# Products of a tile of ones in TensorE's waits, in an encoder trunk of one layer

## What is computed

```python
u = rms_norm(x, attn_norm) @ w_in
y_h = hyena_mixer(u[..., :1536], ...)            # short conv, two long convolutions by FFT, gates
y_a = mla_mixer(u[..., 1536:1792], u[..., 1792:1920], u[..., 1920:], ...)   # 8 heads of attention
y = rms_norm(concatenate([y_h, y_a]).reshape(B, L, 2, 512), out_norm.reshape(2, 512))
x = x + y @ w_out
x = x + ec_moe(rms_norm(x, mlp_norm), w_router, w_gate, w_up, w_down)
```

## Time and profile before

| what | value |
|---|---|
| median of 3 runs | 2699.3 us (2695.45 to 2703.31) |
| the profiled execution's own time | 2694.75 us |
| its span | 2693.0 us |
| TensorE busy | 2466.5 us, 92% of the span |
| mean granted clock of TensorE | 0.949 of full speed |

### The profile page before, as it was taken

One profiled execution on the slowest core, in us unless ns is written; L12 is line 12 of the kernel. 1 busy time (PEld: TensorE's weight loads), 2 busy tenths in 40 slices (PEclk: granted clock), 3 DMA queues, 4 the chain that ended last, 5 costly groups with the idle time before them and its releaser, 6 DMA issues. The chain is left out here.

```text
span 2693.0 us, 50844 instructions
## 1 busy us (share of the span) xinstructions
PE 2466.5 (92%) x19983; PEld 1381.6 (51%) x19983; DVE 1898.6 (71%) x2630; ACT 1640.7 (61%) x2314; POOL 1145.8 (43%) x1032
## 2 busy tenths in 40 slices
PE   6899999879999999998898989799944999999997
PEld 4555555436666666663332233355433666666664
DVE  5547767647777777776898989566646677777773
ACT  6734455338888888887654855343434666666651
POOL 1224344226666666666403900234312355544431
PEclk9999999969999999998899989899965999999999
DMA  7403345344311211125796888755544899999972
GB/s 191 132 34 129 111 141 175 116 86 158 111 41 42 48 41 44 30 53 192 255 331 213 291 285 294 209 160 158 157 148 115 273 270 275 276 259 258 271 189 51
DMA packets 391771, 445.10 MB, mean 165 GB/s; under 512 B 206159, under 2 KB 270415, under 8 KB 389265
## 3 DMA queue, kind: packets, MB, share of 16 engines
q1 hardware_dynamic: 367056, 369.78, 44.9%
q0 software_dynamic: 12288, 38.05, 5.9%
q10 hardware_dynamic: 12224, 34.48, 3.7%
HBM read 267.72 MB, written 137.91 MB: 151 GB/s over the span
## 5 line engine op out<-in xcount | busy, mean ns | idle before, releaser
L1276 POOL TENSOR_TENSOR at_p<-at_pf,at_p 128x512 f16<-128x512 f32 x325 | 378.6, 1173 | 260.7 <-ACT at_p L1411 260.3
L1552 DVE TENSOR_REDUCE at_mxs<-at_pM 128x1 f32<-128x512 f32 x512 | 344.0, 688 | 102.1 <-PE at_pM L1442 100.2
L1410 ACT ACTIVATE at_pf<-at_pS,at_scale 128x1024 f32<-128x1024 f32 x260 | 289.8, 1115 | 107.7 <-PE at_pS L1473 103.1
L1411 ACT ACTIVATE at_p<-at_pS,at_scale 128x1024 f16<-128x1024 f32 x260 | 287.8, 1107 | 0.0
L1498 PE MATMUL at_pO<-at_vv,at_p 128*128 128x65 f16 x2080 | 226.8, 194 | 2.8 <-POOL at_p L1276 2.8
L1499 PE MATMUL at_pO<-at_vv,at_p 128*128 128x64 f16 x2080 | 226.1, 195 | 0.0
L1501 PE MATMUL at_pO<-at_vv,at_p 128*128 128x65 f16 x2080 | 225.6, 193 | 0.0
L1499 PEld LDWEIGHTS at_pO<-at_vv,at_p 128*128 128x128 f16 x2080 | 195.1, 98 | 37.3 <-issue 0.8
L1442 PE MATMUL at_pM<-at_kT,at_qT 96*128 96x512 f16 x512 | 199.3, 391 | 15.6 <-DMA at_qT<-s_QK 12.4
L1498 PEld LDWEIGHTS at_pO<-at_vv,at_p 128*128 128x128 f16 x2080 | 195.2, 97 | 34.6 <-issue 3.0
L1471 PE MATMUL at_pS<-at_qT,at_kT 97*128 97x512 f16 (+1 forms) x528 | 201.5, 382 | 3.3 <-DMA at_qT<-at_nmx 2.2
(11 more groups left out here) (427 smaller groups left out, 6210.1 us busy)
## 6 DMA issues: line engine op xcount, KB each, us to landing
s_F<-fs_a SPq DMA_DIRECT2D x72, 512.0 KB, 3.2
sp_rows<-s_F SPq DMA_DIRECT2D x72, 512.0 KB, 5.7
mo_raw<-in_w_gate SPq DMA_DIRECT2D x32, 1024.0 KB
mo_raw<-in_w_up SPq DMA_DIRECT2D x32, 1024.0 KB
mo_down<-in_w_down SPq DMA_DIRECT2D x32, 1024.0 KB, 5.0
s_QK<-pj_R ACTq DMA_DIRECT2D x18, 1024.0 KB, 3.9
s_G<-sp_gg SPq DMA_DIRECT2D x72, 256.0 KB, 4.3
sp_tab<-tab_spec SPq DMA_DIRECT2D x72, 224.0 KB, 4.2
```

Of the source, the lines that this page charges most:

```text
L1276: eng.tensor_tensor(p2[r][:, half, :], pf[:, r, half, :], p1[r][:, half, :], ALU.subtract).then_inc(own_done if own(g, half) else others_d ...
L1410: act.activation(pf[:, r, :, :], pS[g % 2][:, :, :], ACT.Exp, scale=scale[:, 0:1])
L1411: act.activation(p1[r][:, :, :], pS[g % 2][:, :, :], ACT.Exp, scale=scale[:, 0:1]).then_inc(p_made, 1)
L1552: dve.tensor_reduce(mxs[:, j // NC, j % NC:j % NC + 1], pM[j % 2][:, :], AX.X, ALU.max).then_inc(pM_free, 1)
```

## The change

A helper `keep_awake(pe, out, of, n)` issues `n` products of a tile of ones by itself, 128 x 128 by 128 x 128 in float32, into a PSUM region that nobody reads at that time. None of them signals a semaphore. It runs at 30 points of TensorE's stream and at 13 more in the rounds of `choose` (there with 8 products), and `attend` gets a tile of ones and a semaphore for it. Some of the calls are preceded by a wait for the last reader of the region that they write. Counted over the program it is 965 products. Nothing is removed or moved.

The diff, with the unchanged lines mostly left out:

```diff
--- before.py
+++ after.py
@@ -250,6 +250,12 @@
         TAKEN.append(nc.alloc_semaphore(prefix + name))
...
     return sem
+
+
+def keep_awake(pe, out, of, n):
+
+    for _ in range(n):
+        pe.matmul(out, of[:, :], of[:, :], start=True, stop=True)
 
...
 def clear_semaphores(nc):
@@ -818,10 +824,13 @@
                     last = pe.matmul(pF[:, m, 0:c1 - c0], (w1, w2)[n][:, :], (feats, h1)[n][:, c0:c1], start=True, stop=True)
...
 
+            pe.wait_ge(consts, 4)
+            keep_awake(pe, pC[:, 0:P], ones, 50)
             pe.wait_ge(gain_in, 32)
             turn_x(0)
-            pe.wait_ge(consts, 4)
+            keep_awake(pe, pC[:, 0:P], ones, 10)
             add_squares("c", C_PARTS)
+            keep_awake(pe, pC[:, 0:P], ones, 26)
             turn_x(1)
...
                 if 1 < t + 1 < NT:
@@ -899,6 +908,8 @@
                     make_q(m)
...
                     make_k(m)
+            pe.wait_ge(u_moved, SLOTS)
+            keep_awake(pe, pU[0][:, 0:P], ones, 46)
 
...
         def _(dve):
@@ -1193,6 +1204,7 @@
         q1, q2, k1, k2 = ([x[:, m, :] for x in both] for both in (qT, kT) for m in range(2))
...
         zero = sb("zero", [P, 1])
+        ones = sb("ones", [P, P])
         scale = sb("scale", [P, 1])
...
         mxs = sb("mxs", [P, TQ, NC])
@@ -1207,7 +1219,7 @@
         pS = [ps(f"pS{r}", [P, 2, 512]) for r in range(2)]
...
 
-        consts, eye_in, ready = sem("consts"), sem("eye_in"), sem("ready")
+        consts, eye_in, ready, ones_made = sem("consts"), sem("eye_in"), sem("ready"), sem("ones_made")
         q1_in, q2_in, k1_in, k2_in = ([sem(f"{n}_in{b}") for b in range(2)] for n in ("q1", "q2", "k1", "k2"))
...
         v_in, v_split = sem("v_in"), sem("v_split")
@@ -1364,6 +1376,7 @@
 
...
         def _(pool):
+            pool.memset(ones[:, :], 1.0).then_inc(ones_made, 1)
             pool.memset(zero[:, :], 0.0).then_inc(ready, 1)
...
                 pool.memset(vv[b][:, :, 0:1], 1.0).then_inc(ready, 1)
@@ -1412,6 +1425,8 @@
 
...
         def _(pe):
+            pe.wait_ge(ones_made, 1)
+            keep_awake(pe, pM[0][:, 0:P], ones, 44)
             pe.wait_ge(ready, 3)
...
             def slot(h, b, qb, j):
@@ -1511,6 +1526,7 @@
 
...
                 lead(*leading(0, 0, n))
+            keep_awake(pe, pS[0][:, 0, 0:P], ones, 12)
             for g in range(LAG):
...
             for g in range(NS * NH + NSS):
@@ -1535,6 +1551,8 @@
                         slot(of_h, of_b, of_qb, tiles[2])
...
                     turn_max(of_h, of_qb)
+            pe.wait_ge(pM_free, slots_before(NH, NQ))
+            keep_awake(pe, pM[1][:, 0:P], ones, 38)
 
...
         def _(dve):
@@ -1686,6 +1704,7 @@
             sem("last_in"), sem("topped"), sem("normed"), sem("inverted"))
...
         hidden_in, cleared, z_made, z_moved = sem("hidden_in"), sem("cleared"), sem("z_made"), sem("z_moved")
+        ones_made = sem("ones_made")
         z_out, a_out = ([sem(f"{n}_out{b}") for b in range(2)] for n in "za")
...
         Z_LAG = LAG if closes else 0
@@ -1809,6 +1828,8 @@
         @block.tensor
...
             if order == 0:
+                pe.wait_ge(ones_made, 1)
+                keep_awake(pe, pZ[:, 0, 0:P], s["ones"], 24)
                 pe.wait_ge(hidden_in, 32)
...
 
@@ -1823,6 +1844,8 @@
                     last = pe.matmul(pH[:, d, :], s["hidden"][side, rows(i)], w3[side, :], start=True, stop=True)
...
                 if closes:
+                    if i == 0:
+                        keep_awake(pe, pZ[:, 0, 0:P], s["ones"], 14)
                     pe.wait_ge(g_in[i % GB], 16 * (i // GB) + 16)
...
                         pe.wait_ge(closed, 2 * (i - 2) + 1)
@@ -1878,12 +1901,14 @@
                 if i == NT:
...
             norms(1)
+            pe.wait_ge(z_moved, (1 + closes) * NT)
+            keep_awake(pe, pZ[:, 0, 0:P], s["ones"], 28 if closes else 42)
 
...
             if order == 0:
-                dve.memset(s["ones"][:, :], 1.0)
+                dve.memset(s["ones"][:, :], 1.0).then_inc(ones_made, 1)
 
...
                 dve.memset(s["hidden"][FH:, 0:1], 0.0).then_inc(cleared, 1)
@@ -2122,6 +2147,7 @@
                 last.then_inc(g_made, 1)
...
             pe.matmul(pSum, s["ones"][:, :], s["sizes"][:, :], start=True, stop=True).then_inc(summed, 1)
+            keep_awake(pe, pX[0][:, 0:P], s["ones"], 40)
             pe.wait_ge(totalled, 2)
...
                 forward(n)
@@ -2129,6 +2155,8 @@
                     backward(n - LAG)
...
                 backward(n)
+            pe.wait_ge(x_moved, STEPS)
+            keep_awake(pe, pX[0][:, 0:P], s["ones"], 36 if order else 24)
 
...
         def _(dve):
@@ -2541,10 +2569,13 @@
 
...
             pe.matmul(pW, ones[:, :], w_sum[:, :], start=True, stop=True).then_inc(w_summed, 1)
+            keep_awake(pe, pU[:, 0:P], ones, 15)
             invert(0)
+            keep_awake(pe, pU[:, 0:P], ones, 48)
             pe.wait_ge(eye_in, 16)
...
             invert(1)
+            keep_awake(pe, pU[:, 0:P], ones, 8)
             for t in range(NT):
...
                     invert(t + 2)
@@ -2557,8 +2588,11 @@
                     turn_y(t + 1)
...
                     route(t - 1)
+            pe.wait_ge(chain, 2 * NT)
+            keep_awake(pe, pV[:, 0:P], ones, 28)
             turn_x(NT - 1)
             route(NT - 1)
+            keep_awake(pe, pV[:, 0:P], ones, 28)
 
...
         def _(dve):
@@ -2812,7 +2846,8 @@
         pP = ps("pP", [P, 512])
...
         pO = [ps(f"pO{g}", [P, 512])[:, 0:2 * P].rearrange("p (s b e) -> p s b e", s=2, b=16) for g in range(2)]
-        pF = ps("pF", [P, 512])[:, 0:NC * E_N].rearrange("p (c e) -> p c e", c=NC)
+        pF_bank = ps("pF", [P, 512])
+        pF, spare = pF_bank[:, 0:NC * E_N].rearrange("p (c e) -> p c e", c=NC), pF_bank[:, 0:P]
 
...
         loaded, turned, chain, exps = sem("loaded"), sem("turned"), sem("chain"), sem("exps")
@@ -2866,6 +2901,8 @@
 
...
         def _(pe):
+            pe.wait_ge(consts, 1)
+            keep_awake(pe, spare, weights["ones"], 20)
             pe.wait_ge(loaded, 32)
...
             for n in range(4):
@@ -2909,15 +2946,21 @@
 
...
             pe.wait_ge(consts, 3)
+            keep_awake(pe, spare, weights["ones"], 26)
             for n in range(ROUNDS):
...
                     add_squares(pe, weights, pN[:, 0:W_PARTS], 0)
+                elif n < ROUNDS - 1:
+                    keep_awake(pe, spare, weights["ones"], 8)
             pe.wait_ge(tabs_in, 48)
+            keep_awake(pe, spare, weights["ones"], 20)
             pe.wait_ge(picked, 1)
             rank(tied, tied_sum, over_sum)
+            keep_awake(pe, spare, weights["ones"], 8)
             pe.wait_ge(picked, 2)
             rank(taken, taken_sum, nothing)
+            keep_awake(pe, spare, weights["ones"], 62)
             pe.wait_ge(placed, 1)
...
                 n, of, first, last_t = (P, 0, 0, NP - 1) if t < NP else (H, 1, NP, NP + NS - 1)
@@ -2926,6 +2969,7 @@
                     last = pe.matmul(pO[g][:, of, :, :], in_a[0:n, t, g, :, :].rearrange("p a e -> p (a e)"), in_b[0:n, t, g, :, :],
...
             last.then_inc(spotted, 1)
+            keep_awake(pe, spare, weights["ones"], 14)
             pe.wait_ge(spread_made, 1)
...
                 for g in range(2):
@@ -3442,16 +3486,21 @@
                     add_h(e - 1)
...
                 product(e, b, 1, 0)
-                if not begins(e):
+                if begins(e):
+                    keep_awake(pe, pY[0][:, 0:P], weights["ones"], 28)
+                else:
                     down(e - 1)
...
                 product(e, b, 2, 1)
+                if begins(e):
+                    keep_awake(pe, pY[0][:, 0:P], weights["ones"], 8)
                 if more == 2:
...
                 product(e, b, 3, 1)
+            keep_awake(pe, pG[1][:, 0:P], weights["ones"], 46)
             pe.wait_ge(eye_made, 1)
...
                 at = 2 * CAPS[1] if c == 2 else 0
@@ -3463,6 +3512,8 @@
                     add_squares(pe, weights, pN, 1)
...
             add_h(E_N - 1)
+            pe.wait_ge(y_ready, 2 * NC * (E_N - 1))
+            keep_awake(pe, pY[0][:, 0:P], weights["ones"], 28)
             down(E_N - 1)
```

## The result

The changed kernel takes 2752.7 us (median of 4 runs, 2749.3 to 2755.9), the kernel before 2699.9 us in the same session (4 runs). The ratio is 1.019, 95% interval 1.0166 to 1.0213. I had forecast 2726 us, with a range to 2748: the direction was right, the size was not. The profiled execution of the changed kernel took 2752.57 us, with a span of 2750.8 us.

A forecast was written before the change was run, and what follows sets the result against it. TensorE, busy 92% of the span, was taken to bound the kernel. Costs of 61 us less gains of 33 gave +28 on 2694.75 us: 2723, or 2727 as a median, given as 2726; range 2690 to 2748.

The forecast's parts named there:

- the price of a product: Each inserted float32 product on TensorE: two records, 0.214 us warm and 0.427 us cold.
- The rival of one record: A product is one record of 0.107 to 0.13 us, so nearly every group fits: 25 us faster, 2674; chance 0.12.
- The costs, place by place: Products ending later than what TensorE waits for, at stage starts, ends and inner waits: 61 us in all.
- the 46 of the experts: At the experts' start, 46 products take 9.8 us in a wait of 7.2: +4 us.
- What warm work gives back: TensorE work on the chain that ran at half clock gets faster: 33 us together, of a bound of 70.
- `attend`'s opening: Start of `attend`, 19 us busy at low clock, paced by VectorE's maxima: gain of 4 of at most 9 us.
- the starts of filters, spectra and merge: First steps of `filters`, `spectra` (twice) and `merge` gain about 2.5 us each, second `filters` 1: together 11.
- the rounds and ranks: In `choose`, counts behind the last mask shorten 0.2 us a round, 3 in all; ranks and placings give 4.
- the first expert: TensorE's work in the first expert, run warm, gives back 6 us.
- the last `down`: TensorE's work in the experts' last `down`, run warm, gives back 2.4 us.
- Costs and gains cancel: Transfers that ran ahead make up delays at starts, and `attend` opens warm for 9 us: about 2700; chance 0.12.
- The clock stays low in the rounds: In `choose`, 8 products take 3.4 us in a wait of 1.75, 13 times: 22 us more, 2748; chance 0.08.

The follow-up runs named there:

- the fitted version: Changed kernel with counts sized to the waits of the kernel before, 578 products instead of 965: ratio 0.9991 to the kernel before.
- the four lean versions: Changed kernel cut to some 400 products (0.9983); that without 40 at the seam to `attend` (0.9983); `choose` and last `down` alone (0.9981); some 400 plus 16 in `attend` (0.9979).
- halved version: Changed kernel with half of the products at every place, some 480 instead of 965: ratio 0.9995 to the kernel before.
- the narrow products: Changed kernel with all 965 products over 64 columns instead of 128: ratio 1.0669 to the kernel before.
- the three without these products: Changed kernel with 40 products at the seam to `attend` alone (1.0002), those plus 16 in `attend`'s first block (1.0008), or some 200 in the middle stages alone (0.9997).

## Why the prediction was wrong

- **What bounds the kernel, and the price of a product: right.** TensorE's free time was too small for 965 products. A product costs 0.20 to 0.23 us where nothing hides it, and the rows of float32 work were the right ones. The rival of one record is refuted by the 1930 records, and half the counts and the float16 products show that even it would have gained nothing.
- **The costs, place by place: about right as a sum.** 61 us forecast, and the stages are 57 us longer, costs less gains. No stage is off by more than 2.6 us from its costs alone. Mis-sized terms: the 24 products of the first `filters` (3.7 forecast, 7.0 measured, since the clock fell in the wait for their ones); the 46 of the experts (4 forecast, 6.5 to 8 by leaving them out); `choose` (5.8 forecast, 3.2 measured with its gains in it). The mean wait of 1.75 us in the rounds, into which 8 products "just fit", was misread: one of the 15 waits is 3.9 us, the others are 1.60 on average (22.4 / 14).
- **"What warm work gives back": the step that failed.** With the gains at zero the forecast would have been 2694.75 + 61 = 2756 us; the profiled executions of the changed kernel took 2752.6 and 2754.3 us. Of the 33 us some 4 are left if the costs were as forecast (61 less the 57 of the table), and some 10 if the two dearer terms above are added to them. The versions that hardly delay anything show the gains nearly alone: from none to 6 us (ratios 0.9979 to 1.0008). Of the single terms: `attend`'s opening (4) is real, but not in the products' hands; the starts of filters, spectra and merge (11 together) gave at most 1 us each in the fitted version; the rounds and ranks (7) left `choose` at 77.0 to 78.8 us in the four lean versions, where it was 78.0 to 78.1, with a mean clock of 0.89 in it; the first expert (6) was returned in the wait for ScalarE's squares; the last `down` (2.4) is right: in each fitted, lean or halved version its products took 2.3 us less than in the first trace of the kernel before (1.0 less and 0.5 more in the unchanged kernel's other traces).
- **The error in method.** I took for each cold stretch a part of its busy time, as "what stood on the chain", without a row that shows what ends last there. In most of those stretches the other engines' work and the transfers stand beside TensorE's, and a shorter product only makes it wait longer for them; the first expert shows it, for the starts of the stages it is argued from their lengths. Removing 195 us of half clock changed the time by 0.1%. The Trainium skill, "TensorE: Matmul & The Clock Gate", section "Terms", prices throttled time at one minus the clock's share: 195 x 0.5 = 98 us. This case's runs disagree by far more than I had thought when I set 70 us as the bound.
- **The rivals.** "Costs and gains cancel" (2700) is what the fitted versions do, not this one. "The clock stays low in the rounds": refuted here, and shown to be possible by the narrow products. That delays at starts would be made up by transfers was wrong in the changed kernel.
- **The range** ended at 2748, 22 us above the forecast, so that its upper end still needs some 11 of the 33 us of gains. It should have held the case of none, since no row of the profile showed that one of them would reach the end. The chances too (0.08 for the one rival above 2745) gave that case almost nothing.

Open: the four versions with lean counts in `choose` and ahead of the last `down` are 0.2% faster, about 5 us, and only the last `down` (some 2 us) has a place. Each of their intervals ends below 1, and the three without these products are at 0.9997 to 1.0008. `choose` itself is 1.1 us shorter in one of the four and not in the others. The experts' stage is 627.1 to 631.1 us in the four, and 629.5 to 635.8 in the unchanged kernel and the three, but it varies by 5 us without any change. Whether the rest comes from there, these runs can't tell.

## What to carry to other kernels

Before work is put into an engine's waits to keep its clock up, price both sides in the trace: the filler by the nearest rows, against each wait from its start to the moment at which another engine really ends it, and the gain by what is late next when the engine is faster. How busy the other engines are doesn't tell: at `attend`'s opening VectorE was busy half of the time and TensorE 19.05 of 20.5 us, and a warm clock is worth 6 us; in the first expert TensorE came 3.6 us earlier to a wait for ScalarE, and nothing was gained. And take two or three traces of the unchanged kernel first: stages that differ by 6 us between them can't be forecast, or explained, to 3.

## What the runs showed of the hardware

- A float32 product with 128 x 128 weights takes 0.23 us warm with 64 columns as with 128 (9.12 and 9.18 us for 40). The records of the weight loads are the same in both there (192 ns on average at the starts of `spectra`), which suggests that the loads set the pace. The Trainium skill, "TensorE: Matmul & The Clock Gate", section "LDWEIGHTS (loading the stationary operand)", gives the time of a load in ns as its columns divided by 1.2 and names no clock; for 128 columns that is an estimate of 107 ns. The warm turn of 0.112 us for a record is near it, and the cold one of the narrow products, 0.216 us, is twice that.
- A float16 product of 128 columns is one record and took 0.10 us at the start, nearly all of it at the pace of half clock (4.99 us for 50), where two cold float32 records take 0.43.
- Narrow products kept TensorE busy without pause for 19 us and left the clock at 1.2 GHz; those of 128 columns raised it at the same seam.
- Two executions of one program had the clock at 0.50 and at 1.00 in the same 10 us of the same stage, and the stage differed by 6.3 us.
